# Extra rows of an expert in blocks of 64, with both parts of an operand in one stationary tile

## What is computed

```python
g_val, g_idx = lax.top_k(g_prob, 1)                 # one group of 8 experts for a token
e_val, e_idx = lax.top_k(sel, TOP_K)                # two experts in it
weights = jax.nn.softmax(e_val, axis=-1) * g_val
...
h = jax.nn.silu(xb @ w1[e]) * (xb @ w3[e])          # 1024 -> 512
return h @ w2[e]                                    # 512 -> 1024
```

## Time and profile before

| what | value |
|---|---|
| median of 3 runs | 3073.09 us (3070.35 to 3078.69) |
| profiled execution, span (the page gives no other time of it) | 3070.8 us |
| TensorE busy | 2707.0 us, 88% |
| VectorE, ScalarE, GpSimd busy | 1592.6, 1027.7, 672.0 us |
| mix and merge stages | 0 to about 1917 us |
| routing until the first expert matmul | to 1992.4 us |
| experts | to about 2960 us |
| combine | to 3070.8 us |
| gathers of blocks (L1528) | 51: 49 blocks and 2 ahead |

### The profile page before, as it was taken

The page is one execution under the profiler, slowest core; times in us unless marked ns, Lnnn a source line. Parts: engine busy times, 40 slices in busy tenths (PEclk is TensorE's granted clock), DMA queues, the critical chain, the costliest instruction groups (busy, mean ns, idle before and its releaser), DMA issues. The chain is left out here.

```text
span 3070.8 us, 38499 instructions
## 1 busy us (share of the span) xinstructions
PE 2707.0 (88%) x12616; PEld 1986.9 (65%) x12617; DVE 1592.6 (52%) x2288; ACT 1027.7 (33%) x1259; POOL 672.0 (22%) x537
## 2 busy tenths in 40 slices
PE   4889898986999999999999999299999999998950
PEld 2333333434886788578858884188998889988840
DVE  8867767664334334434443334755445454455448
ACT  2121212202222222222222222155445464456531
POOL 4413132320000000000000000434334333346361
PEclk8989999987999899999999999599999999999985
DMA  5123131307334233423333342388667867679767
GB/s 161 36 78 99 50 120 48 123 21 209 95 101 144 86 95 94 149 85 99 94 138 92 95 126 104 123 301 301 235 233 256 293 226 252 220 260 351 250 259 293
DMA packets 462189, 490.99 MB, mean 160 GB/s; under 512 B 30545, under 2 KB 388177, under 8 KB 462161
## 3 DMA queue, kind: packets, MB, share of 16 engines
q1 hardware_dynamic: 436096, 421.46, 42.0%
q0 software_dynamic: 11952, 43.52, 4.0%
q10 hardware_dynamic: 14112, 25.70, 2.2%
HBM read 415.13 MB, written 75.50 MB: 160 GB/s over the span
## 5 line engine op out<-in xcount | busy, mean ns | idle before, releaser
L1099 PE MATMUL mrgps<-act_hi,w_hi 128*128 128x512 f32 x1280 | 503.8, 394 | 30.2 <-DVE w_lo L1167 23.6
L1099 PE MATMUL mrgps<-act_lo,w_hi 128*128 128x512 f32 x1280 | 502.3, 392 | 0.0
L1099 PE MATMUL mrgps<-act_hi,w_lo 128*128 128x512 f32 x1280 | 501.9, 392 | 0.0
L1584 PE MATMUL exps<-w_hi,xT_hi 128*128 128x256 f32 x1568 | 444.6, 284 | 2.2 <-DVE xT_lo L1675 2.2
L1584 PE MATMUL exps<-w_hi,xT_lo 128*128 128x256 f32 x1568 | 444.8, 284 | 0.0
L1584 PE MATMUL exps<-w_lo,xT_hi 128*128 128x256 f32 x1568 | 444.7, 284 | 0.0
L502 PE MATMUL mixps<-xT,win 128*128 128x512 f32 x896 | 409.1, 612 | 0.8 <-ACT xT L405 0.8
L1443 POOL TENSOR_TENSOR w_lo<-w_raw,w_hi 128x1024 fp32r<-128x1024 f32 x128 | 325.8, 2585 | 220.2 <-ACT w_hi L1434 220.2
L502 PEld LDWEIGHTS mixps<-xT,win 128*128 128x128 f32 x896 | 170.9, 195 | 238.0 <-issue 234.5
L1438 DVE TENSOR_TENSOR w_lo<-w_raw,w_hi 128x2048 fp32r<-128x2048 f32 x124 | 300.0, 2460 | 37.6 <-ACT w_hi L1429 37.6
L1584 PEld LDWEIGHTS exps<-w_hi,xT_hi 128*128 128x128 f32 x1568 | 301.7, 192 | 4.7 <-issue 2.6
(11 more groups left out here) (334 smaller groups left out, 3623.1 us busy)
## 6 DMA issues: line engine op xcount, KB each, us to landing
w_raw<-in_expert_w_dram SPq DMA_DIRECT2D x128, 1024.0 KB, 5.8
w_raw<-in_merge_gate_w_dram SPq DMA_DIRECT2D x132, 512.0 KB, 4.1
w_raw<-in_expert_w_dram SPq DMA_DIRECT2D x32, 2048.0 KB, 9.8
win<-in_w_in_dram SPq DMA_DIRECT2D x56, 512.0 KB, 3.9
expert_rows<-ysb ACTq DMA_DIRECT2D x98, 256.0 KB, 5.1
w_raw<-in_branch_w_dram SPq DMA_DIRECT2D x132, 128.0 KB, 4.0
xin<-in_x_dram SPq DMA_DIRECT2D x20, 512.0 KB, 6.4
act_raw<-xn_feature_major SPq DMA_DIRECT2D x10, 1024.0 KB, 8.2
```

The costliest lines, as they stand in the source:

```text
L1099: last = pe.matmul(bank[:], w[:, k % 2, kk], x[:, a], start=(kk == w_tiles[0] and x is act_hi and w is w_hi), stop=(kk == w_tiles[-1] and ...
L1584: last = pe.matmul(hbank[j][:, w * HC:(w + 1) * HC], x[:, k], wts_part[:, 2 * j + w, cols], start=(k + n == 0), stop=(k == KD - 1 and n == 2))
```

## The change

Rows of an expert beyond its first 128 go in steps of 64. An expert has 1 + ceil((count - 128)/64) blocks, if count is above 128, else 1. Its last block is a full one of 128 rows; the ones before it are half blocks. In a half block the stationary tile holds the 64 low columns beside the 64 high ones (BOTH), so that one matmul with the high weights and one with the low weights do what three did (and low x low besides). The result has 128 rows, 64 of the low part and 64 of the high, which must be added: ScalarE copies rows 64 to 127 from PSUM to hrow, VectorE adds rows 0 to 63 into hs, in SBUF, and tanh, gg and hg read hs. The same is done with the result of the second layer (yrow, ysb). The second layer is cut in two: its first half of f runs ahead of the transposes turn_h(g, 1) and turn_x(g+1, 1). The parts of x and of h lie in one tile of five pieces of 64 columns, low, high, high, low, low, and VectorE writes the first low piece in an instruction of its own, in full blocks too.

Around it: route computes the new places (steps of 64 up to 2048 rows: 30, not 16 steps in `big`; 96, not 66 columns in U and the table matmuls; seven more small steps in its chain, one less). The zeros come in 45 transfers of 64 rows, not 15 of 128, two behind each load of w2. hg is cleared once. For want of semaphores those of the mix stage are cleared and given back ahead of the merge stage. A full block keeps its matmuls; its x is turned and split in two halves.

The core of the diff (signatures, the fills, the semaphores, and moved lines are left out):

```diff
@@ constants
-NB = T * 2 // P + E
+HB = P // 2
+PARTS = 5
+BOTH, HIGH, LOW = slice(0, P), slice(HB, HB + P), slice(HB + P, HB + 2 * P)
+NSTEP = (T - P) // HB
+NB = 94
@@ def route
-            s.link(TTc(big[:], cnt[:].unsqueeze(2).to_broadcast([P, E, TT]), io_blk[:].unsqueeze(1).to_broadcast([P, E, TT]), ALU.is_gt))
+            s.link(TTc(big[:], cnt[:].unsqueeze(2).to_broadcast([P, E, NSTEP]), io_over[:].unsqueeze(1).to_broadcast([P, E, NSTEP]), ALU.is_gt))
...
+            s.mark(dve.tensor_scalar(posq[:], pos[:], HB.bit_length() - 1, RANKS // HB - 1, ALU.logical_shift_right, ALU.bitwise_and))
...
+            s.link(dve.tensor_scalar(backf[:], backf[:], -1.0, 0.0, ALU.add, ALU.max))
+            s.link(dve.scalar_tensor_tensor(backm[:], backf[:], 1.0, backf[:], ALU.min, ALU.add))
+            s.link(TTc(blkf[:], blkf[:], backf[:], ALU.subtract))
+            s.link(dve.scalar_tensor_tensor(slotf[:], backm[:], -float(HB), slotf[:], ALU.mult, ALU.add))
+            s.link(TTc(ei[:], ei[:], blkf[:], ALU.add))
+            s.link(dve.scalar_tensor_tensor(posf[:], ei[:], float(HB), slotf[:], ALU.mult, ALU.add))
@@ def run_experts, TensorE
+            def expand(g, e4, products):
+                for j in range(2):
+                    pe.wait_ge(gated, g * 2 + (j + 2))
+                    for w in range(2):
+                        pe.wait_ge(wt.split13, e4 + (2 * j + w + 1))
+                        for k in range(KD):
+                            cols = slice(k * HC, (k + 1) * HC)
+                            for n, (x, weights) in enumerate(products(xT, k, wt.hi13, wt.lo13)):
+                                last = pe.matmul(hbank[j][:, w * HC:(w + 1) * HC], x, weights[:, 2 * j + w, cols],
+                                                 start=(k + n == 0), stop=(k == KD - 1 and weights is wt.last13))
+                    last.then_inc(h_ps, 1)
+            def contract(g, j, products):
+                pe.wait_ge(h_split, g * 2 + (j + 2))
+                for f in (2 * j, 2 * j + 1):
...
+            def block_products(parts, k, hi, lo):
+                return (parts[:, k, HIGH], hi), (parts[:, k, LOW], hi), (parts[:, k, HIGH], lo)
+            def half_products(parts, k, hi, lo):
+                return (parts[:, k, BOTH], hi), (parts[:, k, BOTH], lo)
+            def half_block(g, e4):
+                pe.wait_ge(x_both, g * 2 + 2)
+                expand(g, e4, half_products)
+                turn_h(g, 0)
+                turn_x(g + 1, 0)
+                pe.wait_ge(wt.split2, e4 + 4)
+                contract(g, 0, half_products)
+                turn_h(g, 1)
+                turn_x(g + 1, 1)
+                contract(g, 1, half_products)
...
@@ run_experts, ScalarE
+            def half_block(g, e):
+                high_rows(g, 0)
+                half_tanh(g, 0)
+                high_rows(g, 1)
+                high_h(g, 0, HB)
+                half_tanh(g, 1)
+                high_x(g + 1, 0)
+                high_h(g, 1, HB)
+                high_x(g + 1, 1)
+                for n in range(2):
+                    act.wait_ge(y_ps, g * 2 + (n + 2))
+                    act.activation(yrow[:, n], ybank[n][HB:P, :], ACT.Copy, scale=0.5).then_inc(y_high_set, 1)
...
@@ run_experts, VectorE
+            def half_gate(g, j):
+                dve.wait_ge(high_set, g * 2 + (j + 1))
+                dve.tensor_tensor(hs[:, j], hbank[j][0:HB, :], hrow[:, j], ALU.add).then_inc(sum_set, 1)
+                dve.wait_ge(tanh_d, g * 2 + (j + 2))
...
+                dve.scalar_tensor_tensor(gg[0:HB, j], th[0:HB, j], 1.0, hs[:, j, 0:HC], ALU.add, ALU.mult).then_inc(gate_d, 1)
+                dve.wait_ge(gate_d, g * 2 + (j + 2))
+                dve.tensor_tensor(hg[0:HB, j], gg[0:HB, j], hs[:, j, HC:2 * HC], ALU.mult).then_inc(gated, 1)
...
+            def half_block(g, e):
+                half_gate(g, 0)
+                half_gate(g, 1)
+                low_h(g, 0, HB)
+                low_x(g + 1, 0)
+                low_h(g, 1, HB)
+                low_x(g + 1, 1)
...
```

More of the change, by code:

```diff
@@ L1485, in expert @@
                     with eng.Fori(b0, last) as g:
-                        block_of(g, None)
-                block_of(last, eng.snap(e + 1) if split else None)
+                        half_block(g, e)
+                block_of(last, e, split)
             with eng.Fori(0, E - 1) as e:
@@ L1528, in gather, with one @@
                 pool.indirect_dma_start(xg[:], None, dram["xn"], bass.IndirectOffsetOnAxis(idx[:], 0)).then_inc(gathered, 16)
-            def one(g, nxt):
+            def half_block(g, e):
                 gather(g + 2)
-                if nxt is not None:
-                    wt.write_low2(pool, nxt)
+            def one(g, e, split):
+                gather(g + 2)
+                if split:
+                    wt.write_low2(pool, pool.snap(e + 1))
             gather(0)
@@ L1541, in _ @@
             gather(1)
-            over_blocks(pool, one)
+            over_blocks(pool, half_block, one)
             total = pool.value_load(ends[0:1, E:E + 1], min_val=1, max_val=NB - 1)
@@ L1549, in _, with turn_x @@
         def _(pe):
[L1550 to L1554 removed]
+            def turn_x(g, h):
+                if h == 0:
+                    pe.wait_ge(gathered, g * 16 + 16)
+                for k in range(4):
+                    last = pe.transpose(tbank[h][:, k * P:(k + 1) * P], xg[:, (4 * h + k) * P:(4 * h + k + 1) * P], ident[:])
                 last.then_inc(turned, 1)
             def turn_h(g, j):
[L1558 removed]
+                pe.wait_ge(gated, g * 2 + (j + 4))
                 for c in range(2):
@@ new lines, in contract @@
+            def contract(g, j, products):
+                pe.wait_ge(h_split, g * 2 + (j + 2))
+                for f in (2 * j, 2 * j + 1):
+                    for c in range(2):
+                        if f == 0:
+                            pe.wait_ge(y_free, g * 2 + (c + 2))
+                        for n, (x, weights) in enumerate(products(hT, f, wt.hi2, wt.lo2)):
+                            last = pe.matmul(ybank[c][:], x, weights[:, f, c * 512:(c + 1) * 512],
+                                             start=(f + n == 0), stop=(f == FE - 1 and weights is wt.last2))
+                        if f == FE - 1:
+                            last.then_inc(y_ps, 1)
@@ L1565, in _, with one @@
+            def one(g, e4):
+                pe.wait_ge(x_split, g * 2 + 2)
+                expand(g, e4, block_products)
+                turn_h(g, 0)
+                turn_x(g + 1, 0)
+                turn_x(g + 1, 1)
+                turn_h(g, 1)
+                pe.wait_ge(wt.split2, e4 + 4)
+                contract(g, 0, block_products)
+                contract(g, 1, block_products)
+            pe.sem_inc(turned, 2)
             pe.sem_inc(h_ps, 1)
@@ L1568, in _ @@
             pe.wait_ge(idn, 1)
-            turn_x(0)
+            turn_x(0, 0)
+            turn_x(0, 1)
             with pe.Fori(0, E) as e:
@@ L1678, in one @@
+            def one(g, e, split):
+                nxt = dve.snap(e + 1) if split else None
                 gate(g, 0)
```

186 lines of the change are left out of this document (97 added, 89 removed).

## The result

The changed kernel takes 3122.37 us (median, 3120.98 to 3123.51), the kernel before 3075.3 us with the runs made beside it: a ratio of 1.0148, 95% interval 1.0132 to 1.0163. The change makes the kernel 1.5% slower. The profiled execution has a span of 3119.8 us, 49.0 more than before.

The account below looks back on a forecast made before the run. TensorE looked the bound, with GpSimd's low part of w2 at its heels (slack 0.87 us). Regular half blocks 0, late ones 3, clock 32 and routing 6 gave +41 on 3073.09 us: 3114 us, range 3072 to 3134.

Parts of the forecast that it names:

- Hold: Half blocks: gg and hg, reading SBUF alone, wait out GpSimd's w2 instruction; second layer 1.7 us later.
- wait: Half blocks: TensorE waits for hg near 3 us ahead of its first pair of transposes, 17 times.
- clock: Half blocks: TensorE idles and its granted clock falls to 0.5; 1.9 us each, 32 us for 17.
- the late blocks: Five half blocks where GpSimd starts w2 late because of the weights' transfers; +3.1 us in all.
- Behind the second layer: Half block, from the second layer's start: 16 matmuls with the turn and split of h's second half between; 4.8 us.
- regular: Twelve half blocks without late weights: 19.1 us each before the clock's cost, the same as before, so 0 gained.
- Rival 1: Half blocks: all as forecast, but TensorE's clock stays at 1.00; +9 us, 3082 us; chance 0.23.
- the fills: 45 transfers of zeros in place of 15, riding with the weights of experts 0 to 22; 0, bound 3 us.
- The routing: Ahead of the expert stage: wider big, U and table matmuls and new small links; +6 us, bounds 4 and 8.
- Rival 2: Half blocks: short instructions find SBUF free, w2 alone limits, 17.4 us a block; 3053 us; chance 0.15.
- Rival 3: Expert stage: TensorE's own work alone counts, -97 + 6 us; 2982 us; chance 0.02.
- Rival 4: Half blocks: clock at 1.2 GHz through the second layer and into the next block, 2.9 each, fills 3; 3134 us; chance 0.08.

Follow-up runs that it names:

- pool_8: The changed kernel with GpSimd's low part of w2 in eight instructions of 512 columns, not four of 1024; 1.0160 times the kernel before.
- psum_sums: The changed kernel with the half blocks' first-result sums written back to PSUM, where tanh, gg and hg read them; 1.0054 times the kernel before.
- busy_idle: The changed kernel with 17 matmuls of discarded result in each half block, where TensorE waits anyway; 1.0055 times the kernel before.
- nb64: The changed kernel with room for 64 blocks, not 94, so 66 columns in U and 15 transfers of zeros; 1.0117 times the kernel before.
- psum_busy: The changed kernel with half-block sums in PSUM and 14 matmuls of discarded result in each half block; 0.9971 times the kernel before.
- high_first_busy: The changed kernel with half-block sums in PSUM, high-part w2 matmuls first in half blocks, and nine discarded matmuls in each; 0.9874 times the kernel before.

## Why the prediction was right, and where it was off

The forecast was 3114 us, +41. Measured were 3122.4 against 3075.3, +47.1 between the medians and +49.0 between the profiled executions. Hold, wait and clock were as forecast; the late blocks were not, and two errors of opposite sign partly cancel.

**A half block up to its second layer.** The steps hold one by one. Measured, and predicted in brackets, from S: first sum until 7.21 (7.2), tanh until 7.67 (7.6), gg until 8.17 (8.2), hg until 10.64 (10.9), first transposes 10.70 (10.95), second sum until 11.25 (11.5), tanh until 12.00 (11.9), gg until 13.14 (13.2), hg until 13.60 (14.0), second layer 13.90 (14.3). The last two are 0.4 early: GpSimd was done at 12.86, and hg followed gg at its 0.46, where I had counted 0.8. The rule that I took from the Trainium skill, SBUF — State Buffer, section SBUF: two separate sides (VectorE with both inputs in SBUF and GpSimd lock each other out for a whole instruction), agrees: 2448 ns at most with both in SBUF, 414 with one in PSUM, 1.37 us in the block of pool_8, where GpSimd's instructions are half as long. Had this rule failed, psum_sums would have measured what the changed kernel did.

**Behind the second layer.** 4.8 us predicted, 5.0 measured in busy_idle. Without the clock a regular half block takes 18.97; I had 19.1 and before it was 19.10. Of the twelve that the prediction called regular, eleven are at 18.95 to 18.98 in busy_idle; the twelfth, of expert 22, had become late.

**The clock.** Predicted 1.9 a block and 32 us, measured 1.82 in a regular block and 28.3 in all. Rival 1 (the clock holds) fell in the profile after: in the block shown TensorE did nothing but six transposes from S+7.8 to S+13.9, and the granted clock was 0.50 from shortly ahead of the first of them until about S+20. busy_idle shows what rival 1 would have been worth, 1.0055 x 3075.3 = 3092 and not 3082.

**The late blocks.** This is the term of the sum that was mis-sized. I had +3.1 us in all, for experts 2, 13, 17, 27 and 29, by how late GpSimd started on w2 in the kernel before. In busy_idle the half blocks of experts 2, 17, 22, 27 and 29 take 1.0, 2.6, 3.0, 1.0 and 1.2 us more than the blocks before, 8.8 in all, and 13 no more than before. I had moved the lateness of before forward, but the weights come later in the changed kernels: GpSimd starts on w2 of experts 17, 22 and 29 at S+5.35, 5.48 and 4.44 in busy_idle, and at S+3.43, 3.10 and 3.19 before. About 2.2 of the 8.8 are the lower clock that busy_idle still has in experts 17, 22 and 27 (an estimate: what these three take, from the first transposes to the second layer and behind it, beyond a regular block). Part of the lateness comes from an edit that I set at nothing with a bound of 3, the fills. nb64 shows it for experts 17 and 22 alone, 1.4 us; for the rest the cause stays open. The full blocks, set at 0, became 5.6 longer, 5.4 of it in experts 12, 24 and 26, single blocks with late weights (24.90, 24.79 and 22.11 us for 23.69, 21.61 and 21.09). Of the 5.4, 1.7 lie ahead of the second layer, which waits for w2, and 3.7 behind its start: around it the granted clock was 0.50 for 6.8 us in the blocks of 12 and 24, where before it was for 3.4 us in 12 and not at all in 24. nb64 gives none of the 5.6 back (626.1), so the fills aren't its cause; which transfer is late there I didn't find.

**The routing.** 6 predicted, 6.55 measured until the first expert matmul, but not for the reasons given. The routing itself grew by 4.3. VectorE and TensorE in it, answering to the earlier trace rows:

```profile
1962.77 1.16 DVE L1380 TENSOR_TENSOR big<-rt_c,io_over 128x960 f32<-128x960 f32 x1
...
1975.06 1.75 DVE L1409 TENSOR_TENSOR U<-io_b,blkf 128x1536 fp32r<-128x1536 f32 x1
...
1984.61 3.49 PEld L1325 LDWEIGHTS rtps<-U,V 128*128 128x128 f32 x16 [2.42 <-DVEq L1411]
1984.62 3.65 PE L1325 MATMUL rtps<-U,V 128*128 128x96 f32 x16 [2.26 <-DVEq L1411]
```

big and U are as computed. The table matmuls aren't: 3.65 us for 96 columns beside 3.62 for 66, where I had added 1.6. The weight loads beside them take 3.48 us for 16 before and 3.49 after, for the same 128 columns each, and leave no gap. So it seems that they set the pace; no run changed them. The other 2.3 us stood already at the start of the routing. There the code differs in a few semaphore instructions only, but the first matmul of the merge stage starts between 716.0 and 724.6 us in the twelve traces of this case, eleven of which have the same code up to there. So these 2.3 are the scatter of the stages before, and part of the agreement with 6 is luck.

**The sum.** Measured, in the order of the prediction: regular half blocks without the clock -1.3, the seven others +8.6, clock +28.3, until the first expert matmul +6.5, full blocks +5.6, the rest +1.2: 49, against +41 (0, 3, 32, 6, and nothing for the last two). Blocks with late weights, half and full, cost 11 us more than forecast; the clock (3.7) and the regular blocks (1.3) made up for part of that. The split isn't sharp: by the estimates above 2.2 + 3.7 us of these 11 are the clock falling in late blocks, so that the clock as a whole cost about 34 us.

**The rivals.** Rival 2 (no hold, w2 alone limits) is what psum_busy makes: 17.65 a block where 17.4 was worked out. Its 3053 would have been 0.9971 x 3075.3 = 3066, again by the late blocks. Rival 3 (TensorE's own work counts, 13.4 a block) isn't reached even by high_first_busy with 15.79: between the layers the chain from the sum through tanh and gates remains. Rival 4 had the clock at 2.9 a block, and no kernel showed that.

## What to carry to other kernels

A change that saves work on the busiest engine is worth what the next limit leaves, and limits that stand behind each other hide one another: here the place of a sum and an order of matmuls were worth 0.9% and 0.1% alone and 2.4% together. When an intermediate result moves from PSUM to SBUF, look for a GpSimd instruction beside its readers: one PSUM operand kept 34 small instructions (a gg and an hg in each of 17 half blocks) from being held, for up to 2 us each. And when TensorE has less to do in a stretch with unchanged waits, read the granted clock there: it made all of the loss in the regular blocks here, and a few matmuls whose result is thrown away gave it back.

## What the runs showed that I had not expected

- The fp32 table matmuls took as long for 96 moving columns as for 66 (3.65 and 3.62 us for 16, at a granted clock of 0.50). Each goes with a load of 128 stationary columns, and 16 of these took 3.48 us before and 3.49 after.
- GpSimd's subtraction of 128x4096 elements took 9.74 us in four instructions and 10.49 in eight, with VectorE instructions held beside both. With nothing held, in psum_sums, four took 9.38.
- The hold seems to work in the other direction too: GpSimd's 9.38 in psum_sums was 9.74 in the changed kernel, where gg and hg read SBUF alone.
